# A hybrid layer with 32 experts on one core: the last w2 loads in single steps, and the final norm shared out between VectorE, ScalarE and GpSimd

## The chip, the cores and the metric

One core of a Trainium2 chip runs the whole layer. The metric is the device time in microseconds of one launch, as the median of several runs. All data are float32 unless a step says otherwise. Below, TensorE, VectorE, ScalarE, GpSimd and SyncE are the core's engines (PE, DVE, ACT, POOL and SP in the rows); each runs its own program in order, and they meet through semaphores.

## What is computed

A decoder layer for 256 prompt tokens, 16 meta tokens in front of them, and 8 sample tokens; the width is 1024. Cut to what matters here:

```python
u = _rmsnorm(tok, norm_mix[l]) @ w_in[l]          # then convolution and recurrence
mix = jnp.concatenate([...]) @ w_out[l]
h = h + mix
ff = _moe(_rmsnorm(h, norm_ffn[l]), router_w[l], ...)   # top 4 of 32 experts

def _moe(x, ...):
    for e in range(N_EXPERTS):
        a = x @ w1[e] + b1[e]
        glu = jnp.minimum(a[:, ::2], 7.0)
        lin = jnp.clip(a[:, 1::2], -7.0, 7.0)
        act = glu * jax.nn.sigmoid(1.702 * glu) * (lin + 1)
        out = out + combine[:, e:e + 1] * (act @ w2[e] + b2[e])

y_prompt = _rmsnorm(h_p + ff_p, norm_final)
y_sample = _rmsnorm(h_s + ff_s, norm_final)

def _rmsnorm(x, g):
    return x * lax.rsqrt(jnp.mean(x * x, axis=-1, keepdims=True) + EPS) * g
```

## The kernel before

After the mixers and the router, the experts are worked through in sixteen pairs. A pair has at most 64 tokens for each of its two experts (`CAP`); TensorE gathers them, multiplies by w1 (L1767), transposes the activations (L1800), multiplies by w2 (L1821) and scatters the result back to all 264 tokens with the gates (`rows`, L1703, and for the last pair `end_rows`, L1716). Each expert's w1 (8 MB) and w2 (4 MB) go through a ring of eight slots of 2 MB. SyncE issues the loads in the order of use, each as soon as `w_used` says that its slot is free; a full load brings four contraction steps of 128 rows of w2 for one expert, 16 KB per partition.

For the last pair the loads are finer: from j = 6 on, each is cut into two halves (`load_half`). The two second halves of the last w2 loads (j = 10 and 11, one for each expert) signal `half_in[2]`. In `pair` TensorE works through the last w2 in groups: with v = 1, part = 0 it takes steps 0 and 1, with part = 1 it waits for `half_in[2]` and takes steps 2 and 3, the left 512 columns of the result first (half 0) and then the right 512 (half 1). A product for one expert and one step and half is two records of 128x512 in the profile. When half 0 is complete, `b_ps` lets ScalarE copy it out of PSUM (L809), then half 1.

`end_rows` then multiplies by the gates: six products in the order of the list `END`, (tile 0, left), (tile 1, left), (samples, left), (samples, right), (tile 0, right), (tile 1, right). Tiles 0 and 1 hold 128 prompt tokens each, the samples are 8 rows. `finish` on VectorE adds each product to h (L1230), `finish` on ScalarE squares each sum with an accumulator (L817) and takes three roots (L824). VectorE does the rest: reciprocals (L1247), and h times the reciprocal root times norm_final as one instruction, for the samples over 1024 columns (L1255) and for each half of a tile (L1252). VectorE's order is written out by hand: sums 0 to 3, three small biases (L1238), sum 4, the samples' reciprocal and result, sum 5, then tile 0 and tile 1. `store_rows` on SyncE waits for each result with `fin_sb` and issues five stores: the samples (L481) and the four halves (L485). GpSimd's last work is the load of norm_final into `gfin`, two pairs before the end.

A later pass over the experts exists for a launch in which an expert has more than 64 tokens (`later_pass`); it isn't run here.

## Time and profile before

| | us |
|---|---|
| median of three runs | 1131.18 |
| lowest and highest run | 1131.0 and 1132.29 |
| the profiled execution's own time | 1131.36 |
| its span, from the first to the last instruction | 1129.5 |
| TensorE busy with products | 1050.4 |
| VectorE busy | 284.8 |
| ScalarE busy | 183.2 |
| GpSimd busy | 26.9 |
| read from and written to HBM | 427.50 MB and 3.48 MB |

The times of the trace are counted from the span's start. The ends of TensorE's products are modelled, and its busy time hides pauses of the pipeline. A group of a timeline is drawn from its first start to its last end.

### The profile page before, as it was taken

What the parts mean: (1) busy time and instruction counts of PE and PEld (TensorE: products, weight loads), DVE (VectorE), ACT (ScalarE), POOL (GpSimd) and SP (SyncE); (2) the same over time, 40 slices, a digit from 0 to 9 for tenths busy, and PEclk for the clock granted to TensorE, in tenths of its full rate; (3) what the DMA queues carried; (4) which work ended last, traced back from release to release, by engine and by line L of the source; (5) the groups of instructions that cost most, each with busy time, mean ns of one, the idle gap of its engine ahead of it and who ended that gap; (6) DMA issues with size and microseconds to landing.
All of it is one profiled execution on the core that took longest, in us unless ns stands there. A gap on an engine that the chain in (4) does not pass through costs nothing.

```text
span 1129.5 us, 13096 instructions
## 1 busy us (share of the span) xinstructions
PE 1050.4 (93%) x5365; PEld 467.1 (41%) x5365; DVE 284.8 (25%) x515; ACT 183.2 (16%) x418; POOL 26.9 (2%) x63
## 2 busy tenths in 40 slices
PE   7999998999999999989899999898989999999996
PEld 6767854343443333424243434342434343433332
DVE  5657535222130202112121212120202020202023
ACT  2562004220210010102020202010101010100103
POOL 3000013000000000000000000000000000000000
PEclk9999999999999999999999999999999999999998
DMA  9942376799999999999999999999999999999993
GB/s 305 359 157 75 139 241 269 312 428 431 426 426 429 427 427 428 429 428 429 428 429 427 428 429 429 429 429 427 428 429 429 429 428 428 428 429 428 427 421 155
DMA packets 50034, 431.46 MB, mean 382 GB/s; under 512 B 5086, under 2 KB 15878, under 8 KB 24304
## 3 DMA queue, kind: packets, MB, share of 16 engines
q1 hardware_dynamic: 47984, 428.15, 91.1%
q0 software_dynamic: 752, 2.56, 0.7%
q10 hardware_dynamic: 1264, 0.28, 0.1%
q8 instruction: 23, 0.38, 0.1%
q14 instruction: 11, 0.09, 0.0%
HBM read 427.50 MB, written 3.48 MB: 382 GB/s over the span
## 4 chain that ended last, share of the span: by engine, by line
PE 56%; DMA 38%; DVE 2%; ACT 1%; issue 1%; SPq 1%; DVEq 0%
DMA ring<-in_expert_w 38%; PE ps L1767 17%; PE ps L1821 16%; PE ps L1402 7%; PE ps L1692 4%; PE ps L1381 2%; PE ps L1528 2%; PE ps L1703 2%; ACT mem L764 1%; PE ps L1470 1%; PE ps L1800 1%; PE ps L1705 1%; DMA ring<-in_x_prompt 1%; SPq L414 0%; PE ps L1390 0%
## 5 line engine op out<-in xcount | busy, mean ns | idle before, releaser
L1767 PE MATMUL ps<-ring,mem 128*64 128x512 f32 x2048 | 461.5, 599 | 51.7 <-DMA ring<-in_expert_w 51.6
L1767 PEld LDWEIGHTS ps<-ring,mem 128*64 128x64 f32 x2048 | 155.1, 137 | 346.4 <-issue 345.5
L1821 PE MATMUL ps<-ring,mem 128*64 128x512 f32 x1024 | 225.3, 594 | 4.8 <-ACT mem L782 1.9
L1211 DVE TENSOR_TENSOR mem<-mem,ps 128x1024 f32<-128x1024 f32 x30 | 36.6, 1221 | 466.9 <-PE ps L1703 431.8
L1821 PEld LDWEIGHTS ps<-ring,mem 128*64 128x64 f32 x1024 | 84.2, 137 | 134.1 <-issue 132.0
L774 ACT ACTIVATE mem<-mem 128x512 f32<-128x512 f32 x32 | 20.2, 630 | 538.2 <-DVE mem L1276 538.2
L1402 PE MATMUL ps<-mem,ring 128*128 128x280 f32 x320 | 80.6, 409 | 1.8 <-DVE mem L899 1.5
L1703 PE MATMUL ps<-mem 128*128 128x512 f32 (+1 forms) x180 | 76.5, 611 | 0.0
L1402 PEld LDWEIGHTS ps<-mem,ring 128*128 128x128 f32 x320 | 61.0, 194 | 19.1 <-issue 3.9
L1276 DVE TENSOR_SCALAR mem<-ps 128x512 f32<-128x512 f32 x32 | 22.1, 691 | 154.0 <-PE ps L1767 154.0
L1692 PEld LDWEIGHTS ps<-mem 128*128 128x128 bf16 x840 | 47.4, 98 | 12.2 <-issue 12.2
L809 ACT ACTIVATE mem<-ps 128x512 f32<-128x512 f32 x32 | 19.1, 597 | 204.5 <-PE ps L1821 204.5
L1692 PE MATMUL ps<-mem 128*128 128x128 bf16 x840 | 50.1, 219 | 0.0
L1703 PEld LDWEIGHTS ps<-mem 128*128 128x128 f32 (+1 forms) x180 | 21.8, 155 | 52.3 <-issue 52.3
L1215 DVE TENSOR_TENSOR mem<-mem,ps 8x512 f32<-8x512 f32 x15 | 10.1, 675 | 113.0 <-PE ps L1703 103.4
L764 ACT ACTIVATE mem<-ps,mem 128x128 f32<-128x128 f32 x120 | 34.3, 369 | 11.3 <-PE ps L1692 11.3
L1528 PE MATMUL ps<-ring,mem 128*128 128x512 f32 x64 | 29.4, 601 | 0.2 <-DVE mem L1014 0.2
L1381 PE MATMUL ps<-ring,mem 128*128 128x512 f32 x64 | 29.1, 597 | 0.0
L1800 PE MATMUL ps<-mem 128*128 128x128 f32 x128 | 23.9, 309 | 2.7 <-ACT mem L764 2.7
L1278 DVE TENSOR_SCALAR mem<-ps 128x512 f32<-128x512 f32 x32 | 21.8, 680 | 0.0
L1800 PEld LDWEIGHTS ps<-mem 128*128 128x128 f32 x128 | 17.8, 209 | 7.4 <-ACT mem L764 5.5
L1284 DVE SCALAR_TENSOR_TENSOR mem<-mem 128x512 f32<-128x512 f32 x32 | 20.8, 688 | 0.5
(286 smaller groups left out, 517.4 us busy)
## 6 DMA issues: line engine op xcount, KB each, us to landing
ring<-in_expert_w SPq DMA_DIRECT2D x184, 2048.0 KB, 26.9
ring<-in_expert_w SPq DMA_DIRECT2D x16, 1024.0 KB, 25.0
ring<-in_w_in SPq DMA_DIRECT2D x6, 2048.0 KB, 22.1
ring<-in_w_out SPq DMA_DIRECT2D x2, 2048.0 KB, 11.9
ring<-in_w_in SPq DMA_DIRECT2D x2, 1024.0 KB, 8.1
ring<-in_state_rec SPq DMA_DIRECT2D x4, 512.0 KB, 10.8
out<-ring SPq DMA_DIRECT2D x4, 512.0 KB, 10.3
out<-mem SPq DMA_DIRECT2D x5, 256.0 KB, 4.8
```

The lines of the kernel that those rows point to most:

```text
L764: last = act.activation(xgT4[:, k, 4 * half + q], ps[:, 6 + half, q * P:(q + 1) * P], ACT.Copy, scale=gffn_q[:, 4 * half + q:4 * half + q ...
L1211: dve.tensor_tensor(h3[:, m], h3[:, m], ps[:, 4 + 2 * m:6 + 2 * m, :].rearrange("p a n -> p (a n)"), ALU.add)\
L1276: dve.tensor_scalar(glu[:, at], psA[:, half * D:(half + 1) * D:2], LIMIT, None, ALU.min)\
L1278: dve.tensor_scalar(lin[:, at], psA[:, half * D + 1:(half + 1) * D:2], -LIMIT, LIMIT, ALU.max, ALU.min).then_inc(lin_sb, 1)
L1381: last = mm(ps[:, bank, :], xT3[:, t, at:at + P], w_sb[g][:, t, :], start=(t == 0), stop=(t == KT - 1))
L1402: last = mm(ps[:, bank, 0:TOK], w_sb[g][:, t, j * P:(j + 1) * P], xT3[:, t, :], start=(t == 0), stop=(t == KT - 1))
L1528: last = mm(ps[:, (6, 4)[i] + n, :], yT3[:, k, TILE_COL[i]:TILE_COL[i] + P], wout_sb[k // 4][:, t, n * 512:(n + 1) * 512], start=(k == 0), ...
L1692: last = mm(out, part_of(m, part, t), oh5[0:r, k, m].rearrange("p e s -> p (e s)"), start=(m == 0 and part == 0), stop=(m == 2))
L1703: last = mm(to, ohgT[:, m * P:m * P + r], ysb[:, at], start=True, stop=not biases)
L1767: done = mm(ps[CAP * e:CAP * e + CAP, b, :], xgT4[:, k, t, CAP * e:CAP * e + CAP], ring[:, slot[e], col:col + HALF], start=False, stop=(t ...
L1800: done = pe.transpose(ps[:, 6 + half, q * P:(q + 1) * P], lin[:, half * HALF + q:(half + 1) * HALF:4], ident)
L1821: done = mm(ps[CAP * e:CAP * e + CAP, 4 + half, :], actT3[:, 4 * v + t, CAP * e:CAP * e + CAP], ring[:, slot[e], col:col + HALF], start=(v ...
```

## The change

It has four parts.

1. The two loads of the last pair's last w2 halves become four: step 2 for both experts signals `half_in[2]`, step 3 for both signals a new semaphore `step_in`. Each brings 4 KB per partition. TensorE takes step 2 for both halves of the result, then step 3 for both halves, and waits for `step_in` ahead of step 3.
2. VectorE does all six sums before any reciprocal.
3. The result of the norm is computed in other places. VectorE keeps the right halves of the two tiles as they were. GpSimd multiplies h by norm_final for the left halves of both tiles and for the samples' two halves (results in `fin3`, four instructions), and then scales the samples by their reciprocal root. VectorE scales the left half of tile 0, ScalarE scales that of tile 1 and issues its store itself. SyncE stores the other four, the samples last (`store_first`). As `fin3` is now written by GpSimd, ScalarE's squares go to other places (`squares`). GpSimd's first multiplication waits for the sixth product of `end_rows`.
4. To have semaphores for this, eight of the kernel's early ones are merged into two, `front_ps` (counted by TensorE) and `prep_sb` (counted by VectorE), with the counts named `XT_DONE`, `GAINS_DONE` and so on.

The later pass keeps the old way but for the order of the sums.

```diff
+        squares = [from_(xT, HALF, HALF * m) for m in range(4)] + [from_(lb2, HALF, HALF * m) for m in range(2)]
...
+        FS_DONE, SUMS_DONE, DECAY_DONE, KHAT_DONE, ROUTER_DONE = range(1, 6)
+        XT_DONE, GAINS_DONE, SPREAD_DONE, CROW_DONE = range(1, 5)
+        prep_sb, front_ps = sem("prep_sb"), sem("front_ps")
...
                 for j0 in (6, 8, 10) if last else ():
-                    for half in range(2):
+                    for half in range(1 if j0 == 10 else 2):
...
+                for t, signal in ((2, half_in[2]), (3, step_in)) if last else ():
+                    for j in (10, 11):
+                        sp.dma_start(ring[:, (LOADS * k + j) % SLOTS, t * D:(t + 1) * D],
+                                     w2_v[i * 4 + 2 * k + j % 2, 1, :, t]).then_inc(signal, 16)
+
+            def store_first():
+
+                for nth, at in ((1, slice(HALF, D)), (2, slice(0, HALF))):
+                    sp.wait_ge(fin_sb, nth)
+                    sp.dma_start(y_prompt[0, 0:P, at], fin3[:, 0, at]).then_inc(out_done, 16)
+                sp.wait_ge(fin_sb, 3)
+                sp.dma_start(y_prompt[0, P:2 * P, HALF:D], fin3[:, 1, HALF:D]).then_inc(out_done, 16)
+                sp.wait_ge(fsample_sb, 1)
+                sp.dma_start(y_sample[:, 0, :], fin3[0:NS, 2]).then_inc(out_done, 16)
...
             pool.dma_start(gfin, norm_final.unsqueeze(0).to_broadcast([P, D])).then_inc(gfin_in, 16)
+            pool.wait_ge(gfin_in, 16)
+            pool.wait_ge(act_sb, 2 * PAIRS)
+            for n in range(4):
+                i, half = END[n]
+                r, at = [P, P, NS][i], slice(half * HALF, (half + 1) * HALF)
+                pool.wait_ge(end_added, n + 2)
+                if i == 0:
+                    pool.wait_ge(end_ps, 6)
+                pool.tensor_tensor(fin3[0:r, i, at], h3[0:r, i, at], gfin[0:r, at], ALU.mult).then_inc(fmul_sb, 1)
+            pool.wait_ge(fmul_sb, 4)
+            pool.wait_ge(fbias_sb, 4)
+            pool.tensor_scalar(fin3[0:NS, 2], fin3[0:NS, 2], frstd[0:NS, 2:3], None, ALU.mult).then_inc(fsample_sb, 1)
...
-                    act.activation(fin3[0:r, i, at], h3[0:r, i, at], ACT.Square,
+                    act.activation(squares[2 * i + half][0:r, :], h3[0:r, i, at], ACT.Square,
...
+                if first:
+                    act.wait_ge(fmul_sb, 2)
+                    act.wait_ge(fbias_sb, 6)
+                    act.activation(fin3[:, 1, 0:HALF], fin3[:, 1, 0:HALF], ACT.Copy,
+                                   scale=frstd[:, 1:2]).then_inc(fleft_sb, 1)
+                    act.wait_ge(fleft_sb, 1)
+                    act.dma_start(y_prompt[0, P:2 * P, 0:HALF], fin3[:, 1, 0:HALF]).then_inc(out_done, 16)
...
                 add(4)
+                add(5)
                 dve.wait_ge(gfin_in, 16)
                 for n0, (n, i) in enumerate(((1, 2), (2, 0), (3, 1))):
                     r = [P, P, NS][i]
-                    if n0 == 1:
-                        add(5)
...
-                    if i < 2:
+                    if first and i < 2:
+                        dve.scalar_tensor_tensor(fin3[:, i, HALF:D], h3[:, i, HALF:D], frstd[:, i:i + 1], gfin[:, HALF:D],
+                                                 ALU.mult, ALU.mult).then_inc(fin_sb, 1)
+                        if i == 0:
+                            dve.wait_ge(fmul_sb, 1)
+                            dve.tensor_scalar(fin3[:, 0, 0:HALF], fin3[:, 0, 0:HALF], frstd[:, 0:1], None, ALU.mult)\
+                                .then_inc(fin_sb, 1)
+                    elif first:
+                        pass
+                    elif i < 2:
...
-                        for half in range(2):
-                            for t in steps:
-                                for e in range(2):
...
-                            if v and half == 0 and steps[-1] == 3:
+                        order = [(half, t) for half in range(2) for t in steps]
+                        if v and part:
+                            order = [(half, t) for t in steps for half in range(2)]
+                        for half, t in order:
+                            if last and v and (half, t) == (0, 3):
+                                pe.wait_ge(step_in, c * 32 + 32)
+                            for e in range(2):
...
+                            if v and (half, t) == (0, 3):
                                 done.then_inc(b_ps, 1)
```

VectorE's program from the third sum of the end on, before (TENSOR_TENSOR are the sums, SCALAR_TENSOR_TENSOR the results of the norm; `end_ps` counts TensorE's products, `frt_sb` the roots):

```order
L1230 TENSOR_TENSOR mem<-mem,ps 8x512 [waits end_ps] x2
L1238 TENSOR_SCALAR mem<-mem 128x1 [waits fsq_sb] x2
L1238 TENSOR_SCALAR mem<-mem 8x1 [waits fsq_sb]
L1230 TENSOR_TENSOR mem<-mem,ps 128x512 [waits end_ps]
L1247 RECIPROCAL mem<-mem 8x1 [waits frt_sb,gfin_in]
L1255 SCALAR_TENSOR_TENSOR mem<-mem 8x1024 [waits fbias_sb]
L1230 TENSOR_TENSOR mem<-mem,ps 128x512 [waits end_ps]
L1247 RECIPROCAL mem<-mem 128x1 [waits frt_sb]
L1252 SCALAR_TENSOR_TENSOR mem<-mem 128x512 [waits fbias_sb]
L1252 SCALAR_TENSOR_TENSOR mem<-mem 128x512
L1247 RECIPROCAL mem<-mem 128x1 [waits frt_sb]
```

and the same stretch with the change:

```order
L1269 TENSOR_TENSOR mem<-mem,ps 8x512 [waits end_ps] x2
L1277 TENSOR_SCALAR mem<-mem 128x1 [waits fsq_sb] x2
L1277 TENSOR_SCALAR mem<-mem 8x1 [waits fsq_sb]
L1269 TENSOR_TENSOR mem<-mem,ps 128x512 [waits end_ps] x2
L1285 RECIPROCAL mem<-mem 8x1 [waits frt_sb,gfin_in]
L1285 RECIPROCAL mem<-mem 128x1 [waits frt_sb,fbias_sb]
L1288 SCALAR_TENSOR_TENSOR mem<-mem 128x512 [waits fbias_sb]
L1292 TENSOR_SCALAR mem<-mem 128x512 [waits fmul_sb]
L1285 RECIPROCAL mem<-mem 128x1 [waits frt_sb]
L1288 SCALAR_TENSOR_TENSOR mem<-mem 128x512 [waits fbias_sb]
```

The sixth sum has moved ahead of the reciprocals, the samples' result is gone, and each tile has one two-input multiplication left; a wait on GpSimd (`fmul_sb`) stands in front of the scaling.

GpSimd's program from its last router step to its end, with the change (before, it ended with the DMA row):

```order
L615 TENSOR_TENSOR mem<-mem 128x1024 [waits mid_sb]
L619 DMA mem<-in_norm_final 128x1024 [waits rows_ps]
L628 TENSOR_TENSOR mem<-mem 128x512 [waits end_added,end_ps,act_sb,gfin_in]
L628 TENSOR_TENSOR mem<-mem 128x512 [waits end_added]
L628 TENSOR_TENSOR mem<-mem 8x512 [waits end_added] x2
L631 TENSOR_SCALAR mem<-mem 8x1024 [waits fbias_sb,fmul_sb]
```

Five instructions are new there, all behind the one that waits for `end_ps`, the sixth product.

TensorE's last w2 groups and the products of the end, with the change (before, the group that waits for `half_in2` was followed by seven more products of w2, without another wait):

```order
L1872 MATMUL ps<-ring,mem 64x512 [waits ring_in7,ring_in6,actT_sb]
L1872 MATMUL ps<-ring,mem 64x512 x7
L1872 MATMUL ps<-ring,mem 64x512 [waits half_in2]
L1872 MATMUL ps<-ring,mem 64x512 x3
L1872 MATMUL ps<-ring,mem 64x512 [waits step_in]
L1872 MATMUL ps<-ring,mem 64x512 x3
L1763 MATMUL ps<-mem 128x512 [waits y_sb]
L1763 MATMUL ps<-mem 128x512
```

The group of eight has become two of four, with a wait between them.

## Rows read from the trace of the kernel before

**Rows 1.** The page: busy tenths of TensorE and of the transfers, 40 slices

```profile
PE   7999998999999999989899999898989999999996
DMA  9942376799999999999999999999999999999993
```

**Rows 2.** Chain of waits from 1085 us on: start, us, what

```profile
1084.72 26.59 DMA ring<-in_expert_w
...
1111.35 3.65 PE ps L1821 x16
1115.01 3.74 PE ps L1716 x8
...
1120.81 1.27 DVE mem L1255
```

**Rows 3.** Timeline of TensorE: start, us, engine line operation, count, idle before

```profile
1105.88 0.14 PEld L1821 LDWEIGHTS ps<-ring,mem 128*64 128x64 f32 x2 [0.29 <-issue]
...
1106.50 0.38 PEld L1821 LDWEIGHTS ps<-ring,mem 128*64 128x64 f32 x4 [0.48 <-issue]
...
1109.31 0.14 PEld L1821 LDWEIGHTS ps<-ring,mem 128*64 128x64 f32 x2 [0.28 <-issue]
...
1111.35 3.65 PE L1821 MATMUL ps<-ring,mem 128*64 128x512 f32 x16 [1.01 <-DMA ring<-in_expert_w]
...
1114.93 5.71 PE L1716 MATMUL ps<-mem 128*128 128x512 f32 x12
```

**Rows 4.** Stretches: PE, PEld, DVE, ACT, POOL busy, clock, DMA share, GB/s

```profile
70.00:72.00 2.00, 2.00 (x12) 1.33 (x11) 2.00 (x7) 1.89 (x7) 0.00 (x0) 1.00 1.02 416
1103.00:1107.00 4.00, 4.00 (x21) 1.50 (x22) 0.68 (x1) 2.71 (x4) 0.00 (x0) 1.00 1.00 418
1107.00:1109.00 2.00, 2.00 (x12) 0.69 (x10) 0.00 (x0) 0.00 (x0) 0.00 (x0) 1.00 0.77 324
```

**Rows 5.** Timeline of ScalarE in the last 20 us

```profile
1113.34 0.60 ACT L809 ACTIVATE mem<-ps 128x512 f32<-128x512 f32 x1 [7.21 <-PE ps L1821]
...
1120.55 0.63 ACT L817 ACTIVATE mem<-mem 128x512 f32<-128x512 f32 x1
...
1121.30 0.29 ACT L824 ACTIVATE mem<-mem 128x1 f32<-128x1 f32 x1
```

**Rows 6.** Timeline of VectorE in the last 20 us

```profile
1119.83 0.69 DVE L1230 TENSOR_TENSOR mem<-mem,ps 128x512 f32<-128x512 f32 x1 [0.20 <-PE ps L1716]
...
1120.81 1.27 DVE L1255 SCALAR_TENSOR_TENSOR mem<-mem 8x1024 f32<-8x1024 f32 x1
1122.02 0.67 DVE L1230 TENSOR_TENSOR mem<-mem,ps 128x512 f32<-128x512 f32 x1
...
1122.79 1.41 DVE L1252 SCALAR_TENSOR_TENSOR mem<-mem 128x512 f32<-128x512 f32 x2
```

**Rows 7.** Groups of GpSimd: count, busy us, mean ns, idle before

```profile
L589 POOL TENSOR_SCALAR mem<-mem 8x1024 f32<-8x1024 f32 x1 | 2.9, 2923 | 19.2 <-DVE mem L1099 19.2
...
L595 POOL TENSOR_TENSOR mem<-mem 128x1024 bf16<-128x1024 f32 x1 | 2.1, 2120 | 0.0
L591 POOL TENSOR_TENSOR mem<-mem 8x1024 f32<-8x1024 f32 x1 | 2.1, 2118 | 0.1
...
L587 POOL MEMSET mem<- 128x1024 bf16 x1 | 1.0, 952 | 0.0
```

**Rows 8.** Groups of VectorE: a scaling of 512 columns from and to SBUF

```profile
L972 DVE TENSOR_SCALAR mem<-mem 128x512 f32<-128x512 f32 x2 | 0.9, 434 | 0.0
```

**Rows 9.** SyncE's stores, and stretches of the last 8 us

```profile
1122.11 0.36 SPq L481 DMA_DIRECT2D out<-mem  x1
...
1122.80:1123.40 0.60, 0.00 (x0) 0.00 (x0) 0.60 (x1) 0.60 (x2) 0.00 (x0) 1.00 0.38 55
...
1124.40:1127.40 3.00, 0.00 (x0) 0.00 (x0) 1.33 (x2) 0.00 (x0) 0.00 (x0) 0.50 0.94 346
1127.40:1128.10 0.70, 0.00 (x0) 0.00 (x0) 0.00 (x0) 0.00 (x0) 0.00 (x0) 0.50 0.14 53
1128.10:1129.50 1.40, 0.00 (x0) 0.00 (x0) 0.00 (x0) 0.00 (x0) 0.00 (x0) 0.50 0.00 0
```

More of the change, by code:

```diff
@@ L274, in build_step @@
                              "logitT_ps")]
-        hi_sb, mid_sb, rest_sb, lo_sb, rows1_sb, pool_parts, router_sc = [
-            sem(n) for n in ("hi_sb", "mid_sb", "rest_sb", "lo_sb", "rows1_sb", "pool_parts", "router_sc")]
+        hi_sb, mid_sb, rest_sb, lo_sb, rows1_sb, pool_parts = [
+            sem(n) for n in ("hi_sb", "mid_sb", "rest_sb", "lo_sb", "rows1_sb", "pool_parts")]
         logit_ps, gate_step, member_sb, pos_ps, count_step, combT_ps, combT_sb = [
@@ L290, in build_step @@
             sem(n) for n in ("b_ps", "end_ps", "end_added", "fsq_sb", "fbias_sb", "frt_sb", "stored")]
+        fmul_sb, fleft_sb, fsample_sb = [sem(n) for n in ("fmul_sb", "fleft_sb", "fsample_sb")]
         STEPS = [(c, l) for c in range(2) for l in range(LEVELS)]
@@ L398, in _ @@
             sp.wait_ge(x_sq, 3)
[L399 removed]
+            sp.wait_ge(front_ps, GAINS_DONE)
             for h in range(HEADS):
@@ L809, in pair, with finish @@
                     act.activation(ysb[:, at], psY[:, at], ACT.Copy).then_inc(y_sb, 1)
-            def finish(c):
+            def finish(c, first=False):
                 def square(n):
@@ L852, in first_pass @@
                 each_pair(act, c, pair, ask=ask)
-                finish(c)
+                finish(c, first=True)
             def later_pass(c):
@@ L921, in _ @@
                 dve.tensor_scalar(kS3[:, h, 0:P0C], f[:, 0:P0C], -1.0, 1.0, ALU.mult, ALU.add).then_inc(kk_sb, 1)
-            dve.wait_ge(gains_ps, 2)
+            dve.wait_ge(front_ps, CROW_DONE)
             dve.tensor_copy(cT4, ps[:, 7, 64:128].rearrange("p (g b i) -> p g b i", g=4, i=2)).then_inc(gains_sb, 1)
             dve.wait_ge(kk_sb, HEADS)
-            dve.tensor_scalar(fS3, kS3[:, :, 0:NS], -1.0, 1.0, ALU.mult, ALU.add).then_inc(fS_sb, 1)
+            dve.tensor_scalar(fS3, kS3[:, :, 0:NS], -1.0, 1.0, ALU.mult, ALU.add).then_inc(prep_sb, 1)
             dve.wait_ge(logf_sb, HEADS)
-            dve.tensor_tensor_scan(sums, chain, logs, 0.0, ALU.mult, ALU.add).then_inc(sums_sb, 1)
-            dve.wait_ge(sums_sb, 1)
+            dve.tensor_tensor_scan(sums, chain, logs, 0.0, ALU.mult, ALU.add).then_inc(prep_sb, 1)
+            dve.wait_ge(prep_sb, SUMS_DONE)
             by_block = [cut(ap[:, 0:8 * P], P) for ap in (decay, sums)]
@@ L1217, in add_rows, with finish @@
                     .then_inc(added, 1)
-            def finish(c):
+            def finish(c, first=False):
                 dve.wait_ge(late_sb, c + 1)
@@ L1338, in first_pass @@
                 each_pair(dve, c, pair, start=1, ask=ask)
-                finish(c)
+                finish(c, first=True)
             def later_pass(c):
@@ L1367, in _ @@
                     last = pe.transpose(to, x3[0:r, i, t * P:(t + 1) * P], ident[0:r, 0:r])
-            last.then_inc(xT_ps, 1)
+            last.then_inc(front_ps, 1)
             pe.wait_ge(gain_in, 80)
-            pe.transpose(ps[:, 7, 0:40], gain_rows, ident[0:40, 0:40]).then_inc(gains_ps, 1)
+            pe.transpose(ps[:, 7, 0:40], gain_rows, ident[0:40, 0:40]).then_inc(front_ps, 1)
             for i in range(3):
@@ L1374, in _ @@
                 last = mm(ps[:, 5, at:at + r], ones[0:r, :], diag[0:r, at:at + r], start=True, stop=True)
-            last.then_inc(spread_ps, 1)
+            last.then_inc(front_ps, 1)
             def rows_of(g, i, half, bank, done):
@@ L1411, in _ @@
                                     ident[0:2 * NS, 0:2 * NS])
-            last.then_inc(gains_ps, 1)
+            last.then_inc(front_ps, 1)
             for h in range(HEADS):
@@ L1816, in pair @@
                         steps = range(2 * part, 2 * part + 2) if last else range(4)
-                        for half in range(2):
-                            for t in steps:
-                                for e in range(2):
-                                    col = t * D + half * HALF
-                                    done = mm(ps[CAP * e:CAP * e + CAP, 4 + half, :],
-                                              actT3[:, 4 * v + t, CAP * e:CAP * e + CAP],
-                                              ring[:, slot[e], col:col + HALF], start=(v == 0 and t == 0),
-                                              stop=(v == 1 and t == 3))
-                                    if half and t == 3:
-                                        done.then_inc(w_used, 1)
-                            if v and half == 0 and steps[-1] == 3:
+                        order = [(half, t) for half in range(2) for t in steps]
[5 more added lines that the diff above has]
+                            for e in range(2):
+                                col = t * D + half * HALF
+                                done = mm(ps[CAP * e:CAP * e + CAP, 4 + half, :],
+                                          actT3[:, 4 * v + t, CAP * e:CAP * e + CAP],
+                                          ring[:, slot[e], col:col + HALF], start=(v == 0 and t == 0),
+                                          stop=(v == 1 and t == 3))
+                                if half and t == 3:
+                                    done.then_inc(w_used, 1)
+                            if v and (half, t) == (0, 3):
                                 done.then_inc(b_ps, 1)
```

44 lines of the change are left out of this document (22 added, 22 removed).

## The prediction

> **What bounds the kernel now.** I read the page's slices first [rows 1]: TensorE is busy for nine tenths or more in nearly every slice and the transfers fill theirs up to the last slice. Nothing the change touches lies there except renamed semaphores (counted in the order of one engine's own program, so each wait still ends with the same instruction). So the question is the last 26 us. The chain of waits [rows 2] gives them: the last w2 load lands at 1111.31 us; sixteen matmul records follow, then the products of the end; then VectorE work, among it the samples' 1.27 us multiplication, leads to the stores and the end at 1129.5.
>
> TensorE in time [rows 3]: a weight load every 0.43 us, each for a pair of records (one product for one expert; two experts make four records, 0.86 us). The group before the last has its last load at 1109.31 and nothing is issued until 1111.35. Between two groups that did not wait the step was 0.62 (1105.88 to 1106.50), so the next group could have begun at 1109.93. The idle time that a finer load can fill is 1111.35 - 1109.93 = 1.42 us. The 3.65 us of work behind the landing do not get shorter, they only move into that gap.
>
> VectorE [rows 6]: its sixth sum (128x512 into h) starts at 1122.02, although TensorE's products are 0.93 us apart (3.74 us for eight records, four products [rows 2]) and the fifth was being added at 1119.83, so the sixth was ready at 1120.76. It stood behind the samples' multiplication: 1.26 us late. GpSimd has nothing to do here. The stores: four of 256 KB, whose data fill the queue from 1124.4 to 1127.4 with stragglers to 1128.1, and the span ends 1.4 us behind the last data [rows 9].
>
> **The change part by part.**
>
> *Renamed semaphores:* nothing, as said above.
>
> *Loads of the last steps.* Two 1 MB loads become four of 512 KB, rows of 4 KB in place of 8 KB. SyncE issues two more; the last was issued 26.59 us before it landed [rows 2], so the issue is free. Rate: a 2 MB load with 4 KB rows ran at 416 GB/s, against 418 for the large rows [rows 4]; I take no cost. At that rate the first pair of steps (1 MB) lands 2.5 us before the last, about 1108.8, and is wanted at 1109.93: 1.1 us to spare.
>
> *TensorE's order.* Step 2, both halves: 1109.93 + 4 x 0.43 = 1111.65. Step 3 has landed at 1111.31, so TensorE doesn't wait any more. The left half of step 3 ends at 1111.65 + 0.86; before, ScalarE's copy started 1.99 us behind a start of four pairs (1.72) [rows 5], so a hop is 0.27: the copy runs from 1112.78 to 1113.38, and with 0.1 for the way back the end products start at 1113.48. TensorE itself is free at 1113.37. The loss of the cover is small: the copy used to be ready a microsecond early and is now last by 0.1. Before, the products began at 1114.93 [rows 3]. **Term 1: -1.45 us**, between -1.0 (if the modelled ends of the records are right, an idle time of 1.01 [rows 3]) and -1.58 (copy hidden).
>
> *VectorE.* The sixth product is ready at 1120.76 - 1.45 = 1119.31 and is added until 1120.0. The samples' multiplication (1.27) is gone from VectorE. ScalarE's squares and roots come 1.45 earlier, the second root ending at 1120.15 [rows 5]; the sixth square (0.63 and 0.2 for its accumulator) and the third root (0.29) end near 1121.3. VectorE: reciprocal 0.15, right half of tile 0 0.70 (1121.1), left half as a plain scaling 0.43 [rows 8] (1121.6), reciprocal and right half of tile 1 at 1122.5; ScalarE scales the other left half meanwhile (0.63) and issues its store from its own queue, so that no store waits behind SyncE. The first store is free at 1121.1 where it was 1123.50. In the profile data begin 0.9 behind that and last 3.7 with the stragglers [rows 9]: 1125.7, plus 1.4: this branch would end at 1127.1, **2.4 us early**. It isn't the last one, by what follows.
>
> *GpSimd.* It gets four multiplications of 512 columns and then the samples' scaling of 1024, in a row, and its first one waits for the sixth product (the wait stands ahead of tile 0, so all five are behind it): start 1119.4. A tensor product of 1024 columns took 2.12 us, with 8 partitions as with 128 [rows 7]; half the columns are 1.06, and I take 1.1 for the fixed part. Four: 4.4, to 1123.8. A step on its own result costs 0.1. The scaling of 8x1024: the one row of the same operation, shape and type took 2.92 [rows 7]. That row read every second element, the new one reads adjacent ones, so it can be cheaper; the bound below is the memset of 1024 columns, 0.95. I take 2.92, the nearest row; it ends at 1126.8. Then SyncE's store: the samples' store was issued 0.03 behind its producer and its data moved from 1122.8 to 1123.4, 1.3 behind the producer; with 1.4 to the span's end: **1129.5**. **Term 2: GpSimd's chain of 7.4 us gives back what terms 1 and the sixth sum gained.** Its range: 1127.6 with the memset's price; and upwards the overlap with VectorE, which no row of before shows for two-input work: nothing as the low bound, and as the high bound every VectorE instruction of these microseconds added to the chain, 0.70 + 0.43 + 0.70 = 1.83, or 2.5 with the sixth sum (0.67 [rows 6]). I take nothing, since no row shows such a loss, and keep 2.5 for the range.
>
> The Trainium skill speaks against this change here. "SBUF — State Buffer" (Who interferes with whom) says that VectorE with two SBUF inputs, or in its fast two-port modes, and GpSimd reading SBUF exclude one another for the whole instruction. By that rule the two right halves and the fast scaling all add to the chain: the high bound above and not the low one. No run here shows it yet. "GPSIMD Engine Reference" (Engine selection) says that one-input work there is roughly at line rate, which would put the scaling near the memset's price and not at 2.92.
>
> *Sum.* The span would end at 1129.5 + 0.0 to 0.1. The profiled execution took 1131.36 with a span of 1129.5, so 1.86 lie around it; it is 0.18 above the median of the runs, 1131.18. The sum gives 1131.4 to 1131.5 for such an execution, **1131.3** as a median. A measurement of this kernel can tell some 0.2% from no change, 2.26 us.
>
> **The rivals.**
>
> *A, GpSimd's chain is shorter.* For: the scaling row was strided, and one-input work at the memset's pace is 0.95. Against: the four products have a firm row and alone take 4.2 to 4.4. With 0.95 the chain ends at 1124.85 and the span at 1127.6, 1129.2 as a median. For the full 2.4 us of the other branch the chain must be under 5.0 us, so the scaling under 0.5; then 1128.8, just over the bound. Much of A therefore still is "no change"; a gain over it also needs a larger gap on TensorE than 1.42.
>
> *B, the two engines block one another.* A GpSimd product holds VectorE's right half off, and VectorE's holds the next product off. Place: between 1119.4 and the end. Price: 1.83, and 2.5 if the sixth sum takes part: the chain of 7.4 becomes 9.2 to 9.9, the span ends at 1131.3 to 1132.0, the median is 1133.0 to 1133.7. It is slower by over 0.2% from a chain of 9.7 us on; with a scaling of 0.95 inside it, the chain is 7.3 again and the time that of the forecast. For: the operations overlap by design. Against: no row. This is the skill's rule as a mechanism.
>
> *C, the split doesn't do what it says:* both steps land together, since all four loads lie in one queue and the engines of the queue finish unevenly (324 GB/s from 1107 on [rows 4]). Then TensorE still starts at 1111.35, term 1 is nought and GpSimd's chain ends 1.4 later: 1132.7 as a median. Against: within each engine the rows come in order, and half of the data lie ahead.
>
> **How the numbers follow.** Forecast (chain of 7 to 8 us, ends between 1130.3 and 1132.2): 0.42. A: 0.28, of it 0.14 over 0.2% faster. B: 0.25, of it 0.13 over 0.2% slower. C: 0.05, of it 0.02 slower. Faster 0.14, same 0.71, slower 0.15. The range takes in A with the memset's price and B with its whole price: 1129.2 to 1133.5.
>
> **What would show it.** Right: the last TensorE wait on a w2 load is gone, end products start near 1113.5, the sixth sum follows its product at once; GpSimd has four spans near 1.1 us and one near 2.9 from 1119.4 on, and the samples' store is issued last, some microseconds behind the others. The chain of waits ends with GpSimd. A shows as a last GpSimd span near 1 us; B as gaps or long spans on GpSimd or VectorE (a 128x512 step over 0.75 us) where both work; C as a TensorE wait that stays until 1111.3. Wrong altogether: a chain that ends with a 128x512 store, or an end more than 2.3 us away from 1129.5.

## The result, and the profile after

| | median, us | from, to | runs | profiled execution, its span |
|---|---|---|---|---|
| before | 1131.64 | 1131.0, 1132.82 | 11 | 1131.36, 1129.5 |
| changed | 1133.74 | 1132.04, 1135.92 | 11 | 1132.04, 1130.2 |

The ratio is 1.0019 with an interval of [1.001, 1.0027]: the changed kernel is slower by about 2.1 us. I had forecast 1131.3 and a range up to 1133.5, so the time lies 0.24 us above the range, next to rival B (1133.0 to 1133.7), which had a chance of 0.25. By the bound that I had set (0.2%, 2.26 us) it is still hardly told from no change; by its interval it is slower.

The changed kernel's profiled execution was the quickest of its eleven, with a span only 0.7 us longer than that of before. Two spans can't be set against one another directly here, as the TensorE rows show. This is the changed kernel's timeline of TensorE and of its weight loads (columns as in [rows 3]):

```profile
1101.46 10.52 PE L1872 MATMUL ps<-ring,mem 128*64 128x512 f32 x48
1111.91 5.71 PE L1763 MATMUL ps<-mem 128*128 128x512 f32 x12
...
1110.95 0.14 PEld L1872 LDWEIGHTS ps<-ring,mem 128*64 128x64 f32 x2 [0.29 <-issue]
1111.91 0.30 PEld L1763 LDWEIGHTS ps<-mem 128*128 128x128 f32 x2 [0.81 <-ACT mem L841]
```

All 48 records of the last four w2 steps run without a wait; in [rows 3] the last sixteen waited for their load. But they also began at 1101.46, and in the kernel before at 1103.25, as this line of its timeline shows:

```profile
1103.25 7.09 PE L1821 MATMUL ps<-ring,mem 128*64 128x512 f32 x32
```

The 1.8 us between the two starts arose earlier, in a part where the change only renames semaphores: a wait of TensorE on a w1 load ended at 1081.71 before and at 1079.90 now. Over all the kernels below, which all have the renamed semaphores, the start lay anywhere between 1101.46 and 1104.86, on both sides of that of before. So from here on I cut the end of a trace in two at fixed points:

- from the first w2 record of that row to the start of the end's products: 11.68 us before (1103.25 to 1114.93), 10.45 now (1101.46 to 1111.91). The wait is gone and 1.23 us are gained;
- from that start to the end of the span, called **the distance** below: 14.57 us before (1114.93 to 1129.5), 18.29 now (1111.91 to 1130.2). 3.72 us are lost.

Together this makes +2.5 us, where the medians say +2.1. The chain of waits of the changed kernel tells where the second piece ends (start, us, what):

```profile
1101.53 10.45 PE ps L1872 x48
1111.98 5.66 PE ps L1763 x12
...
1117.81 0.65 POOL mem L628
1118.46 0.58 issue
1119.04 4.77 POOL mem L628 x3
1123.81 0.04 issue
1123.85 2.90 POOLq L63
```

The last row (POOLq) is GpSimd's own sequencer in the time of the scaling.

In [rows 2] the chain left TensorE for VectorE. Now it leaves it for GpSimd, and stays there: four products (L628), the samples' scaling, the samples' store. Its timeline:

```profile
1117.81 6.00 POOL L628 TENSOR_TENSOR mem<-mem 128x512 f32<-128x512 f32 x4 [87.13 <-PE ps L1763]
1123.91 2.84 POOL L631 TENSOR_SCALAR mem<-mem 8x1024 f32<-8x1024 f32 x1
```

Four products in 6.00 us are 1.5 us each, and I had put 1.1. They are not alike: one by one they took 1.26, 1.71, 1.44 and 1.70 us. VectorE in the same microseconds:

```profile
1117.66 0.69 DVE L1269 TENSOR_TENSOR mem<-mem,ps 128x512 f32<-128x512 f32 x1 [0.17 <-PE ps L1763]
...
1118.87 0.75 DVE L1288 SCALAR_TENSOR_TENSOR mem<-mem 128x512 f32<-128x512 f32 x1
1119.54 1.49 DVE L1292 TENSOR_SCALAR mem<-mem 128x512 f32<-128x512 f32 x1
1120.94 0.15 DVE L1285 RECIPROCAL mem<-mem 128x1 f32<-128x1 f32 x1
1121.13 1.56 DVE L1288 SCALAR_TENSOR_TENSOR mem<-mem 128x512 f32<-128x512 f32 x1
```

The sixth sum (1117.66) now follows its product at once, as forecast. The plain scaling of 512 columns takes 1.49 where [rows 8] had 0.43, and the second right half 1.56 where the first took 0.75. Two instructions of this stretch have doubled or tripled; the reciprocal between them has not. The starts show an order in it. The first right half began at 1118.87, the second product 0.17 us after it at 1119.04: the right half kept its 0.75, the product took 1.71. The scaling began at 1119.54, inside that product, and took 1.49. The later starter was the one that took longer, unless the other was nearly done: the first right half itself began in the last 0.2 us of the first product and lost nothing. The stores' transfers aren't needed to explain it: the first of their data moved at 1120.49. The last store and the stretches behind it (columns as in [rows 4]):

```profile
1126.78 0.34 SPq L496 DMA_DIRECT2D out<-mem  x1
```

```profile
1126.78:1127.40 0.62, 0.00 (x0) 0.00 (x0) 0.00 (x0) 0.00 (x0) 0.00 (x0) 0.50 0.00 0
1127.40:1128.20 0.80, 0.00 (x0) 0.00 (x0) 0.00 (x0) 0.00 (x0) 0.00 (x0) 0.50 0.33 51
1128.20:1130.20 2.00, 0.00 (x0) 0.00 (x0) 0.00 (x0) 0.00 (x0) 0.00 (x0) 0.50 0.00 0
```

No data move from 1128.2 on, and the span ends 2.0 us later; in [rows 9] it was 1.4 (1.5 by the single packets). So three things are longer than I put them: a product, VectorE and GpSimd beside one another, and the tail of the store.

### The profile page after: what moved, and what is told of

It reads as the page before. It is cut to its first block, busy times and chain, and to the rows that moved or that the text cites. A ratio compares the mean times of both kernels' runs of the same rounds, so it can differ in the third digit from the quotient of the medians.

```text
span 1130.2 us, 13107 instructions
## 1 busy us (share of the span) xinstructions
PE 1049.8 (93%) x5365; PEld 465.4 (41%) x5365; DVE 284.6 (25%) x513; ACT 183.8 (16%) x419; POOL 35.8 (3%) x68
## 3 DMA queue, kind: packets, MB, share of 16 engines
HBM read 427.50 MB, written 3.48 MB: 381 GB/s over the span
## 4 chain that ended last, share of the span: by engine, by line
PE 58%; DMA 36%; ACT 2%; DVE 1%; issue 1%; SPq 1%; POOL 0%; POOLq 0%; DVEq 0%
DMA ring<-in_expert_w 35%; PE ps L1814 18%; PE ps L1872 17%; PE ps L1449 7%; PE ps L1739 4%; PE ps L1428 2%; PE ps L1575 2%; PE ps L1750 2%; ACT mem L796 1%; PE ps L1517 1%; PE ps L1847 1%; PE ps L1752 1%; DMA ring<-in_x_prompt 1%; PE ps L1763 1%; SPq L420 0%
```

## The experiments

The theory that I took into them: the loads' split gains what it was to gain; GpSimd's chain of five instructions is the new end, it is long by itself, and it is made longer by VectorE working beside it (rival B). Against it: the split loads themselves cost something on the queue or on TensorE; or the new instructions are just slow, and VectorE has nothing to do with it. Every edit is against the changed kernel. The ratios and the last column refer to runs of the kernel before that were taken together with the kernel of that row.

| kernel | median | ratio to before, interval | distance | against before by the trace | by medians |
|---|---|---|---|---|---|
| changed | 1133.74 | 1.0019 [1.001, 1.0027] | 18.29 | +2.5 | +2.1 |
| e1, loads alone | 1130.29 | 0.9984 [0.9975, 0.9993] | 14.59 | -1.2 | -1.5 |
| e2, end alone | 1135.55 | 1.0033 [1.0021, 1.0045] | 18.31 | +3.7 | +3.8 |
| e3, VectorE waits | 1134.56 | 1.0025 [1.0015, 1.0034] | 18.88 | +3.1 | +2.8 |
| e4, samples on VectorE | 1131.16 | 0.9992 [0.9983, 1.0002] | 14.93 | -0.9 | -0.6 |
| e5, products early | 1129.47 | 0.9986 [0.9977, 0.9995] | 14.25 | -1.6 | -2.0 |
| e6, e5 and scaling on VectorE | 1130.0 | 0.9986 [0.9977, 0.9995] | 14.23 | -1.6 | -1.5 |
| e7, sums first, no GpSimd | 1130.13 | 0.9989 [0.998, 0.9998] | 14.75 | -1.1 | -1.3 |
| e8, changed once more | 1134.5 | 1.0027 [1.0018, 1.0037] | 18.32 | +2.5 | +3.0 |
| e9, tile by tile | 1128.89 | 0.9978 [0.9968, 0.9988] | 13.43 | -2.4 | -2.7 |
| e10, e9 without GpSimd | 1129.85 | 0.9982 [0.9973, 0.9991] | 14.41 | -1.4 | -1.8 |

The fifth column is the distance less 14.57, less the 1.23 of the loads in every kernel but e2 (from the first of the last w2 records to the products of the end it took 10.45 or 10.46 us in all of those, 11.70 in e2 and 11.68 in the kernel before). It agrees with the medians within about 0.5 us everywhere. The intervals of the medians are about 1 us wide to each side, so the differences below 1 us are read from the distances.

### e1: the loads' part alone

```
-            pool.wait_ge(gfin_in, 16)
...
-            pool.tensor_scalar(fin3[0:NS, 2], fin3[0:NS, 2], frstd[0:NS, 2:3], None, ALU.mult)
...
-                finish(c, first=True)
+                finish(c)
...
-                add(5)
...
+                    if n0 == 1:
+                        add(5)
...
-                store_first()
+                store_rows(c)
```

> The changed kernel with the old end: VectorE does the samples and both halves of the tiles as before, GpSimd nothing; only the finer last loads and TensorE's order by steps are left (and the squares' other places). If the loads do what the prediction says, the end products start 1.2 to 1.5 us behind the last-but-one group as the changed kernel's profile shows it, nothing is lost behind them, and the time is 1.2 us under the kernel before (1130.4). If the finer loads are themselves what costs (4 KB rows, two more issues), the time is at or over that of before.

Measured: 1130.29, 1.5 us under before. TensorE's timeline:

```profile
1104.86 10.52 PE L1861 MATMUL ps<-ring,mem 128*64 128x512 f32 x48
1115.31 5.71 PE L1752 MATMUL ps<-mem 128*128 128x512 f32 x12
```

The 48 records run through even where the weights came latest of all these executions, and the distance is that of before (14.59 against 14.57). The split does what it says; rival C is dead, and neither the four loads in place of two nor the renamed semaphores, which this kernel has too, cost anything that can be seen.

### e2: the end's part alone

```
-                    for half in range(1 if j0 == 10 else 2):
+                    for half in range(2):
-                for t, signal in ((2, half_in[2]), (3, step_in)) if last else ():
...
-                        if v and part:
-                            order = [(half, t) for t in steps for half in range(2)]
-                            if last and v and (half, t) == (0, 3):
-                                pe.wait_ge(step_in, c * 32 + 32)
```

> The changed kernel with the old loads and the old order on TensorE; the new end is kept. Theory 1 (GpSimd's chain is the end): the loads' gain of 1.2 us is missing, so 1.2 us over the changed kernel, about 3.3 us over the kernel before (1134.9), with GpSimd's chain again near 8.9 us. Rival (the new end is neutral and the finer loads cost 2 us): the time is that of the kernel before.

Measured: 1135.55, 3.8 us over before, with the old wait back and the new distance:

```profile
1109.90 3.65 PE L1864 MATMUL ps<-ring,mem 128*64 128x512 f32 x16 [1.02 <-DMA ring<-in_expert_w]
1113.49 5.71 PE L1759 MATMUL ps<-mem 128*128 128x512 f32 x12
...
1119.38 6.00 POOL L624 TENSOR_TENSOR mem<-mem 128x512 f32<-128x512 f32 x4 [88.68 <-PE ps L1759]
1125.48 2.84 POOL L627 TENSOR_SCALAR mem<-mem 8x1024 f32<-8x1024 f32 x1
```

So the two parts add up: -1.5 and +3.8 make +2.3, and the whole is +2.1. The loss is all in the end, with the same 6.00 and 2.84 as in the changed kernel.

### e3: VectorE waits until GpSimd's products are done

```
+                    if first and i == 0:
+                        dve.wait_ge(fmul_sb, 4)
```

> VectorE waits for all four of GpSimd's products before its first right half, so the products run with nothing beside them. Theory 1 (the two engines exclude one another while both take inputs from SBUF): the four products take 4.2 to 4.5 us instead of 6.0, and VectorE's scaling of 512 columns 0.43 instead of 1.49, unless it meets GpSimd's scaling; what meets that one shows as a lengthened VectorE step. Theory 2 (GpSimd's products are just slower here than in the middle of the kernel): they take 6.0 us again. The time is between 1 us under and 1 us over the changed kernel in both, since VectorE now starts 3 us later: the spans decide.

Measured: 1134.56 (0.8 above the changed kernel's 1133.74, the distance 18.88 against 18.29). For GpSimd and VectorE:

```profile
1119.62 4.92 POOL L628 TENSOR_TENSOR mem<-mem 128x512 f32<-128x512 f32 x4 [87.58 <-PE ps L1765]
1124.64 2.93 POOL L631 TENSOR_SCALAR mem<-mem 8x1024 f32<-8x1024 f32 x1
```

```profile
1125.02 1.27 DVE L1290 SCALAR_TENSOR_TENSOR mem<-mem 128x512 f32<-128x512 f32 x1 [4.37 <-POOL mem L628]
1126.21 0.47 DVE L1294 TENSOR_SCALAR mem<-mem 128x512 f32<-128x512 f32 x1
...
1126.80 0.75 DVE L1290 SCALAR_TENSOR_TENSOR mem<-mem 128x512 f32<-128x512 f32 x1
```

With VectorE silent the four products take 4.92 and not 6.00: 1.08 us of the changed kernel's chain are VectorE's doing, and 0.5 of what I missed there (4.92 against 4.4) is not. Each product took 1.25 or 1.26 us, the second to the fourth no more than the first. VectorE's two lengthened instructions fall back to 0.47 and 0.75 as soon as no product runs beside them, and its first right half, which began 0.4 us after GpSimd's scaling, takes 1.27 in place of 0.75. So the lengthening follows the neighbour and not the instruction. It doesn't last as long as the neighbour, though: the 0.47 and the 0.75 also lie within GpSimd's scaling (1124.64 to 1127.57), so the scaling held off only the first of three instructions. The time doesn't improve, since VectorE's results are now 3 us (the last) to 5 us (the first) later, and their stores are issued at 1126.32 to 1127.61, ahead of the samples': this run shows the cause of the 1.08 us, not their worth.

### e4: the samples' multiplication back on VectorE, last

```
-            for n in range(4):
+            for n in range(2):
...
-            pool.tensor_scalar(fin3[0:NS, 2], fin3[0:NS, 2], frstd[0:NS, 2:3], None, ALU.mult)
...
+                if first:
+                    dve.scalar_tensor_tensor(fin3[0:NS, 2], h3[0:NS, 2], frstd[0:NS, 2:3], gfin[0:NS],
+                                             ALU.mult, ALU.mult).then_inc(fin_sb, 1)
```

> GpSimd has only the two left halves' products; the samples are one VectorE instruction of 1.27 us again, but as its last one, and their store waits for it. Theory 1: GpSimd's 8.9 us chain is gone from the end; the last result is ready about 5.5 us behind the sixth product instead of 8.9, so some 3 us under the changed kernel: 1130.2 to 1130.8, under the kernel before. If the GpSimd chain isn't what ends last in the typical run, the time stays within 1 us of the changed kernel.

Measured: 1131.16, 0.4 above what I had expected, and a distance of 14.93.

```profile
1121.70 1.49 DVE L1289 TENSOR_SCALAR mem<-mem 128x512 f32<-128x512 f32 x1
...
1123.96 1.27 DVE L1302 SCALAR_TENSOR_TENSOR mem<-mem 8x1024 f32<-8x1024 f32 x1
```

Three of GpSimd's five instructions gone from its chain give back 3.4 of the 3.7 us: the chain's length was the loss. What I had left out is that a collision stays as long as GpSimd has any product in these microseconds (the scaling still takes 1.49, 1.0 above its own 0.48), and that is now on the path, because VectorE ends the kernel.

### e5: GpSimd's products as soon as their sums are there

```
                 pool.wait_ge(end_added, n + 2)
-                if i == 0:
-                    pool.wait_ge(end_ps, 6)
+                if n == 1:
+                    pool.wait_ge(end_ps, 1)
```

> The changed kernel, but GpSimd's first product doesn't wait for the sixth product of the end: it starts behind the first sum, and the second one waits for the first end product alone (its place holds the activations until the w2 products are done). From e3, a product alone is 1.23 us. Theory 1 (exclusion only between instructions that both read two inputs, or the fast form, from SBUF; the sums read one input from PSUM): the four products take 4.9 to 5.2 us from 2.1 us behind the start of the end products, so they are done at 7.0 to 7.3, as VectorE begins its first right half; GpSimd's scaling then meets VectorE as in e3. Last result 10.1 us behind the start of the end products in place of 14.8, the span's end 13.5 to 13.9 behind it in place of 18.3: 4.5 us under the changed kernel, about 1129.4, and 2.4 under the kernel before. Rival (GpSimd slows the sums too): a sum takes over 0.75 us and the squares and roots come later by that.

Measured: 1129.47 for an expected 1129.4; the distance is 14.25, over what I had put (13.5 to 13.9), so the median agrees better than its reasoning. GpSimd, then VectorE:

```profile
1114.75 4.96 POOL L628 TENSOR_TENSOR mem<-mem 128x512 f32<-128x512 f32 x4 [83.60 <-PE ps L1763]
1119.82 3.56 POOL L631 TENSOR_SCALAR mem<-mem 8x1024 f32<-8x1024 f32 x1
```

```profile
1118.40 0.69 DVE L1269 TENSOR_TENSOR mem<-mem,ps 128x512 f32<-128x512 f32 x1 [0.17 <-PE ps L1763]
...
1120.28 0.48 DVE L1292 TENSOR_SCALAR mem<-mem 128x512 f32<-128x512 f32 x1
...
1120.86 1.33 DVE L1288 SCALAR_TENSOR_TENSOR mem<-mem 128x512 f32<-128x512 f32 x1
```

One wait moved is worth 4.07 us of the distance (18.32 in e8 to 14.25). GpSimd's first product no longer waits for TensorE's sixth, and the four products run beside VectorE's sums. There they don't disturb one another: 4.96 for four, as when VectorE was silent, and 0.69 for a sum, as everywhere. The sums read one operand from PSUM. The collision has moved to the samples' scaling (3.56, where it took 2.84 in the changed kernel; it began 0.2 us after the first right half, which kept its 0.75) and to the second right half (1.33). The plain scaling between the two took its usual 0.48.

### e6: e5, with the samples' scaling on VectorE as its last instruction

```
+                if n == 1:
+                    pool.wait_ge(end_ps, 1)
...
-            pool.tensor_scalar(fin3[0:NS, 2], fin3[0:NS, 2], frstd[0:NS, 2:3], None, ALU.mult)
...
+                    dve.wait_ge(fmul_sb, 4)
+                    dve.tensor_scalar(fin3[0:NS, 2], fin3[0:NS, 2], frstd[0:NS, 2:3], None, ALU.mult)
```

> As e5, and the samples' scaling of 8x1024 is VectorE's last instruction instead of GpSimd's. Nothing of GpSimd is left beside the right halves: VectorE's steps 0.75, 0.45, 0.75 and 0.7 us, the last result 9.7 to 9.9 us behind the start of the end products, the span's end 13.3 to 13.7 behind it: 0 to 0.4 us under e5, 1129.2.

Measured: 1130.0 for an expected 1129.2, and a distance of 14.23, where 13.3 to 13.7 was expected. The collisions are gone:

```profile
1121.53 0.75 DVE L1285 SCALAR_TENSOR_TENSOR mem<-mem 128x512 f32<-128x512 f32 x1
1122.20 0.48 DVE L1289 TENSOR_SCALAR mem<-mem 128x512 f32<-128x512 f32 x1
...
1123.46 0.73 DVE L1303 TENSOR_SCALAR mem<-mem 8x1024 f32<-8x1024 f32 x1
```

and the last result is ready 9.62 us behind the start of the end's products, against 10.79 in e1 and 10.73 in e5. Yet the end doesn't come sooner, and the stretches say why:

```profile
1123.00:1124.00 1.00, 0.00 (x0) 0.00 (x0) 1.00 (x2) 0.57 (x1) 0.00 (x0) 1.00 0.83 313
1124.00:1125.00 1.00, 0.00 (x0) 0.00 (x0) 0.19 (x1) 0.00 (x0) 0.00 (x0) 1.00 1.02 385
1125.00:1126.00 1.00, 0.00 (x0) 0.00 (x0) 0.00 (x0) 0.00 (x0) 0.00 (x0) 0.65 1.09 367
```

The four stores of 256 KB fill the transfers for three microseconds whatever the engines do. The first of them was ready 7.71 us behind the start of the products and the end follows 6.5 behind that (in the kernel before 6.0, with the samples' store ahead of the large ones). In e5 the first large result was ready at the same 7.71 and the last one 1.1 us later than here, and the distance is the same (14.25). In e5 the two bounds happen to meet: its last result at 10.73 and the 3.52 us behind it also give 14.25. Here the last result would allow an end near 13.1 (9.62 and the 3.45 of the changed kernel), and the end comes at 14.23: the time of the first large result sets it, not that of the last.

### e7: both late sums ahead of the reciprocals, no GpSimd

```
                 add(4)
                 add(5)
                 dve.wait_ge(gfin_in, 16)
...
-                finish(c, first=True)
+                finish(c)
```

VectorE and ScalarE finish as in e1, and GpSimd's five instructions are gone as there.

> e1 (finer loads, all results on VectorE as before) with the six sums first: the sixth sum no longer stands behind the samples. The prediction counted its 1.26 us of delay as a gain. If it is one by itself, 1.2 us under e1. If VectorE's own work is the bound there (sums and results in a row, one instruction's place given to another), the last result stays 10.8 us behind the start of the end products and the time is that of e1 within 0.4.

Measured: 1130.13 against e1's 1130.29, a distance of 14.75 against 14.59. I had counted 1.26 us for the sixth sum standing behind the samples' multiplication. It is worth nothing:

```profile
1118.90 0.69 DVE L1257 TENSOR_TENSOR mem<-mem,ps 128x512 f32<-128x512 f32 x1 [0.17 <-PE ps L1751]
...
1119.68 1.27 DVE L1290 SCALAR_TENSOR_TENSOR mem<-mem 8x1024 f32<-8x1024 f32 x1
...
1122.59 1.41 DVE L1287 SCALAR_TENSOR_TENSOR mem<-mem 128x512 f32<-128x512 f32 x2
```

VectorE has no gap from the sixth sum to its last result; moving the sum ahead of the multiplication changes the order of a full list and not its length. The last result is 10.85 us behind the start of the products, and 10.79 in e1.

### e8: the changed kernel once more

> The changed kernel once more on this chip, unchanged: 2 us over the kernel before, and a profile whose end products to the span's end is 18.3 us as in the first; where the two profiles differ is in when the weights had arrived, not behind it. If the distance itself varies by a microsecond or more, the engines' collision is what scatters the runs.

Measured: 1134.5, a distance of 18.32 against 18.29, with 6.00 and 2.84 us again on GpSimd. The collision doesn't scatter. What scatters from one execution to the next lies ahead of the last w2 records (they began at 1101.46 in the first profile and at 1102.92 in this one).

### e9: tile by tile

The six products of the end go row tile by row tile (both halves of tile 0, of tile 1, then the samples) in place of left halves, samples and right halves. GpSimd keeps two left products only, both in the time of VectorE's sums.

```
-        END = [(0, 0), (1, 0), (2, 0), (2, 1), (0, 1), (1, 1)]
+        END = [(0, 0), (0, 1), (1, 0), (1, 1), (2, 0), (2, 1)]
...
+            pool.wait_ge(end_ps, 1)
+            for i in range(2):
+                pool.wait_ge(end_added, 2 * i + 2)
+                pool.tensor_tensor(fin3[:, i, 0:HALF], h3[:, i, 0:HALF], gfin[:, 0:HALF], ALU.mult)
...
+                add(3)
+                result(0, slice(HALF, D))
+                add(4)
```

> The finer loads, and the end by tiles: TensorE's six products in the order tile 0 left, right, tile 1 left, right, samples left, right, so that tile 0 is complete after two of them. VectorE does the right halves, the left half's scaling of tile 0 and the samples (1.27 us, last); ScalarE the other left half; GpSimd only the two left products, started behind their sums. If what bounds the end of e5 and e6 is when the first large result is free (its four stores need 3.7 us of data and 1.4 behind), the first result is ready 5.6 us behind the start of the end products in place of 7.7 and the last at 9.7; the span ends 13.2 to 13.6 behind that start (14.2 in e5 and e6, 14.6 before): 1128.8, 2.7 under the kernel before. If VectorE's work is the bound instead, it is at 14.0 or over and the time that of e5.

Measured: 1128.89 for an expected 1128.8, a distance of 13.43. GpSimd, VectorE and SyncE:

```profile
1115.70 1.27 POOL L619 TENSOR_TENSOR mem<-mem 128x512 f32<-128x512 f32 x1 [82.06 <-PE ps L1758]
1117.22 1.27 POOL L619 TENSOR_TENSOR mem<-mem 128x512 f32<-128x512 f32 x1 [0.25 <-DVE mem L1254]
```

```profile
1118.20 0.83 DVE L1273 SCALAR_TENSOR_TENSOR mem<-mem 128x512 f32<-128x512 f32 x1
...
1122.20 1.27 DVE L1273 SCALAR_TENSOR_TENSOR mem<-mem 8x1024 f32<-8x1024 f32 x1
```

```profile
1119.06 2.84 SPq L497 DMA_DIRECT2D out<-mem  x3
1123.50 0.34 SPq L499 DMA_DIRECT2D out<-mem  x1
```

The first result is ready 5.46 us behind the start of the products (1119.03) and its store leaves at once, so the stores are spread over four microseconds and the small one comes last. The last result is ready 9.90 us behind the start, 0.3 later than in e6, and the end follows 3.53 us behind it, about as in the changed kernel (3.45): the last result sets the end again. This kernel beats both: by 2.7 us the one before and by 4.9 the changed one.

### e10: e9 without GpSimd

```
-            pool.wait_ge(end_ps, 1)
...
+                result(0, slice(0, HALF))
...
+                result(1, slice(0, HALF))
```

GpSimd's two left products go, and so do VectorE's plain scaling and ScalarE's left half, in whose place VectorE makes both left halves in one multiplication each.

> As e9 with nothing on GpSimd: VectorE computes all four halves and the samples. It does 0.25 and 0.75 us more than in e9: last result at 10.6, the span's end 14.0 to 14.3 behind the start of the end products: 1129.6. If GpSimd's help is given back by collisions, e10 equals e9.

Measured: 1129.85 for an expected 1129.6, a distance of 14.41. The first large result was ready 5.37 us behind the start, even a little sooner than in e9, but the last at 10.73. So GpSimd's two products, put beside VectorE's sums, which read PSUM, and the half that ScalarE scales after them, are worth 0.98 us of distance. The order by tiles alone is worth little (14.41 against 14.59 in e1), and so are GpSimd's early products without it (14.25 in e5): e9's 13.43 has both. The idea of the change, work for the idle GpSimd, was sound; the amount and the moment were not.

## Why the prediction was wrong, point by point

**Term 1, the loads: right.** -1.45 forecast between -1.0 and -1.58; 1.23 by the trace, 1.5 by the medians of e1. The late sixteen records no longer wait, and ScalarE's copy is the last thing before the products, as forecast.

**The sixth sum: seen right, priced wrong.** It now follows its product at once, but the 1.26 us that it stood behind were no gain by themselves (e7). In a list without gaps only what leaves the list counts; the samples' 1.27 us did. This sat in the branch that wasn't to end last, so it cost the forecast nothing.

**GpSimd's chain: the right bound, with three terms too small.** All in us behind the start of the end's products, my numbers from the prediction, measured ones from the changed kernel:

| step | forecast | measured |
|---|---|---|
| first product starts | 5.92 | 5.90 |
| scaling starts | 10.42 | 12.00 |
| scaling ends | 13.32 | 14.84 |
| span ends | 16.02 | 18.29 |

1. *"half the columns are 1.06, and I take 1.1 for the fixed part."* A product of 512 columns alone takes 1.23 (four in 4.92, e3). Only the 1024-column form stood in [rows 7]; twice 1.23 less 2.12 leaves a fixed part of 0.34 for each, where my 1.1 leaves 0.08. Over four: 0.5 us.
2. *"I take nothing, since no row shows such a loss."* The engines do hold one another off: 1.08 us for GpSimd (6.00 against 4.92). This is rival B's mechanism, and the step where the choice failed: between the bounds of nothing and 1.83 I took the one that no row supported either. The Trainium skill's "SBUF — State Buffer" (Who interferes with whom) had said so, and this trace agrees: beside GpSimd's products the second right half (1.56) and the plain scaling (1.49) lengthened, the sums with one PSUM operand (0.69) did not.
3. *"its data moved from 1122.8 to 1123.4, 1.3 behind the producer; with 1.4 to the span's end"*. It is 3.45 and not 2.7 for this last store: 0.75 us. The 1.4 was read behind four large stores, and it is 2.0 behind this small one: 0.6 us. The other 0.15 is a misreading of [rows 9]: 1123.4 is where the window ends, and the packets end at 1123.56, 1.5 us behind the producer, as they do in the changed kernel.

The scaling itself was right (2.84 for 2.92), and so was the start. Sum of the misses: 0.52 + 1.08 + 0.75, less 0.08 for start and scaling, is 2.27 us, which is the 18.29 against 16.02. With the 0.22 us that term 1 fell short (1.23 for 1.45) this is 2.5 us by the trace: the sum's 0.0 became +2.5. By the medians a forecast of +0.1 became +2.1.

**Rival A: dead.** Reading adjacent elements made the scaling hardly cheaper (2.84 against the strided 2.92 of [rows 7]). The Trainium skill's "GPSIMD Engine Reference" (Engine selection) puts one-input work roughly at line rate. These traces disagree: the scaling of 8x1024 took 2.84 on GpSimd and 0.73 on VectorE (e6), and on GpSimd it is dearer than a product of two inputs with as many columns (2.12 in [rows 7]).

**Rival B: the right side, in part for other reasons.** Its price for the blocking (1.83 to 2.5) was too large, 1.08 measured (VectorE lost another 1.8 us beside it, off the path that ended last); the fixed part and the store's tail make up the rest. The split of the losses into these three is shown for the blocking (e3) and for the product alone (e3, e5, e6); the tail is read in every kernel whose last store is the samples'.

**The range.** Both unknown costs stood in it one at a time: the end of the range was B's price on top of a chain otherwise taken at its likeliest values, and the two small terms had no upward bound at all. It even ended 0.2 short of B: B's own upper value is 1133.7, the range that was said to hold its whole price stops at 1133.5, and the result of 1133.74 lies just above both. With 0.5 and 0.75 added to B's 1133.7 it would have reached to about 1135.

## What to carry to other kernels

Before work is given to an idle engine, add up what it does one after another and ask when its first instruction may start: here five instructions in a row behind one late wait cost 3.7 us, and the same ones with the wait moved (e5) cost nothing. GpSimd is best given its SBUF work in the stretches in which VectorE reads PSUM: there four products took 4.96 us and not 6.00. In the last microseconds look at the first large store and at the last result: in e6 the first set the end, in e9 and e10 the last. And each term that rests on a single far row needs an upward bound of its own, all of them added.

## What the runs showed of the hardware

- VectorE and GpSimd lengthen each other, and the later starter is the one that takes longer. VectorE's plain scaling of 128x512: 0.48 alone, 1.49 when it began inside a GpSimd product. Its two-input product of the norm: 0.75 alone or when it began ahead of a GpSimd instruction (which then took longer), 1.56 when it began early inside a product, 0.83 with 0.3 us of the product left (e9). GpSimd's four products: 4.92 alone, 6.00 beside them. VectorE's sums with a PSUM operand stay at 0.67 to 0.69, and the products beside them at 4.96 for four.
- GpSimd's scaling of 8x1024, with one SBUF input, takes part, but not over its whole length: 2.84 alone, 3.56 when it began 0.2 us after a right half (e5). A right half took 1.27 and 1.33 as the first of its kind behind the scaling's start (e3, e5), but in e3 the two instructions after it, still within the scaling, took their usual 0.47 and 0.75.
- A small last store is dear. From the end of the samples' result to the end of the span it took 3.45 us in the changed kernel, 3.48 in e2 and e8, 3.52 in e5, 3.53 in e9, 3.68 in e10 and 3.77 in e4, for 32 KB. Where nothing else moved any more (changed, e2, e8, e10), the last data came 1.5 us behind the result and the span ended 2.0 to 2.2 us behind the data; behind four large stores (before, e1, e7) it ended 1.5 to 1.6 us behind the data. What these 2.0 us consist of was not followed; this stays open.
- The start of the last w2 records scatters by 3.4 us between executions (1101.46 to 1104.86), while the distance behind it repeats to 0.03 us where a kernel was profiled twice or an end was the same (18.29, 18.31, 18.32; 14.57, 14.59). For an edit at the end of a long kernel, distances from a fixed point say more than spans or a few medians.
